# Gated recurrence: the products of k with the carried decays on GpSimd, those of q on VectorE

## The chip, the cores and the metric

One core of one Trainium2 chip runs the whole program. The metric is the device time of one execution in microseconds (us). The kernel before took 1620.99 us, the median of three runs (1618.9 to 1622.72).

## The reference, cut to what matters

The program is two blocks of two layers each in fp32, on 256 tokens and a width of 1024. The change lies in layer 0 of the second block, in a gated linear recurrence with 6 heads of 128 channels:

```python
f = lb[l] + (1.0 - lb[l]) * sigmoid(f_raw);  q = silu(q_raw);  k = 1.0 - f
# per head: S_t = diag(f_t) S_{t-1} + k_t v_t^T,   o_t = S_t^T q_t, chunkwise:
scores = einsum('bhtd,bhsd,bhtsd->bhts', q, k, decay)   # decay = exp(c_t - c_s), s <= t
o = einsum('bhts,bhsv->bhtv', scores, v) + einsum('bhtd,bhdv->bhtv', q * exp(c), state)
```

Beside it, and independent of it until the output product, the same layer attends to 256 memory tokens with 4 heads: `qm = rms_norm(split_heads(qm_raw)) * gain`, softmax of `qm km^T`, and the product with `vm`.

## The kernel before, in words

Five engines run a program each, in a fixed order that the list `schedule()` gives: every engine goes through the same list of stages and does its own part of each. They meet at semaphores: `mark(key)` counts one up when an instruction ends, and `wait_ge(*at(key))` holds the engine until that count is there. An engine works strictly in order; what stands behind a waiting instruction waits too.

The recurrence is computed without a scan, by doubling. Products with TensorE are taken at seven levels s = 1, 2, 4, ... 64. At level s the tokens fall into pairs of neighbouring blocks of s; the scores between the right block's q and the left block's k are what this level contributes. So that one plain product gives them, q carries the decay from the start of its block and k the decay to the end of its block. After each level both are carried on to blocks of 2s: the q of each right block (buffer `hX`) is multiplied by the total decay of its left neighbour, the k of each left block (buffer `hk`) by the total decay of its right neighbour. The totals (`spans`) are ready before the first level.

One level (`("hg_level", s)`) goes thus:

- TensorE, `st_hg_level` (L1434): waits for `("hX", s)`, then 12 head-chunks of scores into three PSUM banks, marked `("hl", s, 0..2)`. All matmuls are recorded at L804 (the helper `mm`).
- VectorE, `st_hg_level` (L2701): waits for `("hl", s, 2)`, since it overwrites what TensorE has just read, then `carry(s)` (L2676): one product for q (L2681), one for k (L2682), each 128 x 768 elements, in place; the mark `("hX", 2s)` is on the second of them. At the last level each has 128 x 384 elements (L2686, L2687). Then six masked copies (L2717) put the three banks' scores into `ST`.
- GpSimd had no part in it.

Between the levels the list puts other work of the layer, `fill[s]`, ahead of `hg_level(s)`: projections `("pa", ...)`, which need about 6 us of TensorE, before levels 2, 4, 8 and 32; the normalisation of the memory queries, `("memq", 0)`, ahead of the projection before level 8; the scores of the memory attention, `("att", "e0", 0)` before level 16 and `("att", "e0", 1)`, with `("sm", "e0", 0)`, before level 32; and transposes and the product with v, `("pt", "e0", 0)` and `("pv", "e0", 0)`, before level 64.

`memq` goes over four engines: ScalarE evacuates the projected queries, GpSimd squares them (L2818, 128 x 512), TensorE sums the squares with a product against ones (the first instruction of TensorE's part, in front of the projection `("pa", "i", 2)`), ScalarE takes the inverse root, VectorE scales (L2620). In the list `memq` stands directly behind `hg_level(4)`.

The memory attention's softmax is VectorE's row maximum (`st_att`, L2397, L2402), ScalarE's exponentials, VectorE's reciprocal and scaling (`st_sm`, L2412, L2415), then TensorE's transposes (`st_pt`, L1186). In VectorE's order these stand between the levels: `att e0 0`, `hg_level(16)`'s carry comes after it, and `att e0 1` and `sm e0 0` behind that.

Weights arrive by DMA from the SP queue; ScalarE and VectorE split each weight into a high part and a rest (L1518, L2075) for TensorE. These splits stand in the same stages.

Of the kernel before, what the change touches and what calls it, by code (L numbers as in the profile page):

```python
# [19 lines left out]
ALU = mybir.AluOpType  # L20
# [3 lines left out]
P = 128  # L24
S = 256
# [7 lines left out]
H_H = 6  # L33
# [3 lines left out]
LEVELS = [1, 2, 4, 8, 16, 32, 64]  # L37
# [315 lines left out]
def two_blocks(nc, w, out, old):  # L353
# [46 lines left out]
    with ctx:  # L400
# [7 lines left out]
        def at(key):  # L408

            return old.at[key] if old.at else ("counting", 1)  # L410

        def sb(name, shape, dtype=F32):
            return ctx.enter_context(nc.sbuf_tensor(name, shape, dtype))
# [22 lines left out]
        def C(name, rows=P):  # L436
            a, b = CONST[name]
            return const[0:rows, a:b]
# [14 lines left out]
        def view(*dims, at=None, parts=False):  # L453
            n = int(np.prod(dims))
            if at is None:
                at = top[0]
                top[0] += n
                assert top[0] <= ARENA, top[0]
            v = (arena_parts if parts else arena)[:, at:at + n]
            names = "abcd"[:len(dims)]  # L460
            if len(dims) > 1:
                v = v.rearrange(f"p ({' '.join(names)}) -> p {' '.join(names)}", **dict(zip(names[1:], dims[1:])))
            return v
# [48 lines left out]
        hh, hl = (sb(n, [P, 2, 2, S], F32R) for n in ("hidden_high", "hidden_rest"))  # L512
# [21 lines left out]
        spans = view(6 * S)  # L534
        hk = view(6, S)
        kf = view(6, S, at=top[0])
        vf = view(NT, 768, at=top[0] + 6 * S)
        hE = view(6, S)
        hX = view(6, S)
# [87 lines left out]
        def bcast(ap, n):  # L627
            return ap.unsqueeze(2).to_broadcast([ap.shape[0], ap.shape[1], n])

        def over(ap, n):  # L630
            return ap.unsqueeze(1).to_broadcast([ap.shape[0], n, ap.shape[1]])
# [130 lines left out]
        def _(eng):  # L762
            pe = Steps(eng, "pe", sems, new)
# [39 lines left out]
            def mm(o, a, b, first=True, last=True):  # L803
                return eng.matmul(o, a, b, start=first, stop=last)  # L804
# [600 lines left out]
                ins.then_inc(*pe.mark(st))  # L1405

            def st_hg_kdT(st):
                pe.wait_ge(*at(("hX", P)))
                for g, (a, n) in enumerate(((0, 4), (4, 2))):
                    b = group(("kdT", g))  # L1410
                    for h in range(n):
                        ins = eng.transpose(b[:, h * P:h * P + P], hk[:, a + h, 0:P], ident)
                    ins.then_inc(*pe.mark(("kdT", g)))
# [20 lines left out]
            def st_hg_level(st):  # L1434
                s = st[1]
                pe.wait_ge(*at(("hX", s)))
                for g in range(3):
                    b = group(("hl", s, g))
                    for i in range(4):
                        n, h = divmod(4 * g + i, 6)  # L1440
                        if s == LEVELS[-1]:
                            ins = mm(b[0:64, i * P + 64:i * P + P], hk[:, h, n * P:n * P + 64], hX[:, h, n * P + 64:n * P + P])
                            continue
                        for d in (0, 64):
                            c = n * P + d
                            ins = mm(b[d:d + 64, i * P + d:i * P + d + 64], hk[:, h, c:c + 64], hX[:, h, c:c + 64])
                    ins.then_inc(*pe.mark(("hl", s, g)))
# [610 lines left out]
        def _(eng):  # L2058
            dv = Steps(eng, "dve", sems, new)
            TTs, TS, STT = eng.tensor_tensor, eng.tensor_scalar, eng.scalar_tensor_tensor  # L2060
# [615 lines left out]
            def carry(s):  # L2676

                left, right = totals(s)
                (kl, _), (_, qr_) = halves(hk, s), halves(hX, s)
                if s < LEVELS[-1]:  # L2680
                    TTs(qr_, qr_, bcast(left, s), ALU.mult).then_inc(*dv.mark())  # L2681
                    TTs(kl, kl, bcast(right, s), ALU.mult).then_inc(*dv.mark(("hX", 2 * s)))  # L2682
                    return
                by_head = lambda v: v.rearrange("p (h n) -> p h n", h=H_H)
                q, k = hX[:, :, P + s:S], hk[:, :, 0:s]
                TTs(q, q, bcast(by_head(left)[:, :, 1], s), ALU.mult).then_inc(*dv.mark())  # L2686
                TTs(k, k, bcast(by_head(right)[:, :, 0], s), ALU.mult).then_inc(*dv.mark(("hX", 2 * s)))  # L2687

            def st_hg_d(st):
                for g in range(3):  # L2690
# [68 lines left out]
        @block.gpsimd  # L2759
        def _(eng):  # L2760
            po = Steps(eng, "pool", sems, new)
            po.stage("init")
            eng.memset(small[:, 510:511], EPS).then_inc(*po.mark())
            po.wait_ge(*po.last())
            eng.memset(small[:, 511:512], float(-0.5 * np.log(128.0))).then_inc(*po.mark())
            po.wait_ge(*po.last())
            eng.memset(small[:, 509:510], float(-np.log(8.0))).then_inc(*po.mark())
            po.wait_ge(*po.last())
            eng.memset(lf, 0.0).then_inc(*po.mark(("consts",)))
            po.wait_ge(*po.last())  # L2770
            eng.memset(cin[:, :, 0:3], 0.0).then_inc(*po.mark(("pads", 0)))
            po.wait_ge(*po.last())
            eng.wait_ge(sems("const_in"), 16)
            T = eng.tensor_tensor
            for st in sched:
                kind = st[0]
                po.stage(kind, st)
                if kind == "norm" and st[1] == "n1":
                    po.wait_ge(*at(("outp_x", "h0")))
                    eng.memset(cin[:, :, 0:3], 0.0).then_inc(*po.mark(("pads", 1)))  # L2780
                    po.wait_ge(*po.last())
                elif kind == "l2":
                    _, l, half = st
                    for p in (2 * half, 2 * half + 1):
                        po.wait_ge(*at(("silu", l, p // 2)))
                        if p >= 2:
                            po.wait_ge(*at(("l2", l, p - 2)))
                        c = cq[:, 2 * p:2 * p + 2, :]
                        T(sq[:, p % 2], c, c, ALU.mult).then_inc(*po.mark(("sq", l, p)))
                        po.wait_ge(*po.last())  # L2790
                elif kind == "mla_norm":
                    l = st[1]
                    for j in range(2):
                        po.wait_ge(*at(("mqkv", l, "mq", j)))
                    po.wait_ge(*at(("mqkv", l, "mkv", 0)))
                    T(qp, mqkv, mqkv, ALU.mult).then_inc(*po.mark(("msq", l, 0)))
                    po.wait_ge(*po.last())
                elif kind == "gdn_a" :
                    _, l, n = st
                elif kind == "tri":  # L2800
                    _, l, n, s = st
                    po.wait_ge(*at(("AT", l, n)))
                    if s == 2:
                        po.wait_ge(*at(("T", l, n, 1)))
                    elif s > 1:
                        po.wait_ge(*at(("U", l, n, s // 2)))
                    else:
                        po.wait_ge(*at(("lhs", l)))
                    T(AM[:, n], AT[:, n], over(C(f"level{s}"), 4), ALU.mult).then_inc(*po.mark(("AM", l, n, s)))
                elif kind == "memke":  # L2810
                    l = st[1]
                    po.wait_ge(*at(("kmr", l)))
                    T(sq2[:, 0], km, km, ALU.mult).then_inc(*po.mark(("mksq", l)))
                    po.wait_ge(*po.last())
                elif kind == "memq":
                    l = st[1]
                    po.wait_ge(*at(("qmr", l)))
                    T(sq2[:, 1], qm, qm, ALU.mult).then_inc(*po.mark(("mqsq", l)))  # L2818
                    po.wait_ge(*po.last())
                elif kind in ("fox_q", "fox_k"):  # L2820
                    z = kind[-1]
                    buf = qf if z == "q" else kf
                    for p in st[1:]:
                        po.wait_ge(*at(("pb" if z == "q" else "pk", z, "raw", p)))
                        if p >= 2:
                            po.wait_ge(*at((f"f{z}n", p - 2)))
                        elif z == "q":
                            po.wait_ge(*at(("mqn" if p else "mkn", 1)))
                        c = buf[:, 2 * p:2 * p + 2, :]
                        T(sq2[:, p % 2], c, c, ALU.mult).then_inc(*po.mark((f"f{z}sq", p)))  # L2830
                        po.wait_ge(*po.last())
# [27 lines left out]
```

## Time and profile before

| | |
|---|---|
| median of 3 runs | 1620.99 us (1618.9 to 1622.72) |
| profiled execution | 1624.74 us, its span 1623.0 us |
| TensorE matmul busy | 1563.7 us, 96% of the span |
| VectorE busy | 1126.3 us, 69% |
| ScalarE busy | 890.7 us, 55% |
| GpSimd busy | 67.4 us, 4%, 58 instructions |
| mean granted TensorE clock | 0.986 of full speed |

The profiled execution took 1.74 us more than its span, from the first to the last instruction, and 3.75 us more than the median of the runs. PE is TensorE, DVE VectorE, ACT ScalarE and POOL GpSimd. A row of a timeline gives start and duration in us, engine, line and operation, output and input, and in brackets how long the engine sat idle before it and on whom it waited. The levels of the recurrence lie between 787 and 838 us of the span.

### The profile page before, as it was taken

How to read it: one execution, taken by the hardware profiler on the slowest of the kernel's cores; microseconds unless marked ns; L12 is line 12 of the kernel's file. 1: busy time of each engine (PE TensorE's matmuls, PEld its weight loads, DVE VectorE, ACT ScalarE, POOL GpSimd, SP SyncE). 2: the span in 40 equal slices, each digit the busy share in tenths (PEclk: the TensorE clock that was granted, in tenths of full speed). 3: DMA queues.
4: the chain of work that ended last, by engine and by line, in shares of the span. 5: the costliest groups of instructions: out<-in, count | busy, mean ns of one | idle time of the engine just before them, and what ended most of it. 6: DMA issues, size and time to landing. Idle time of an engine off the chain costs nothing.

```text
span 1623.0 us, 25818 instructions
## 1 busy us (share of the span) xinstructions
PE 1563.7 (96%) x10654; PEld 1374.6 (85%) x10654; DVE 1126.3 (69%) x1759; ACT 890.7 (55%) x1413; POOL 67.4 (4%) x58
## 2 busy tenths in 40 slices
PE   7999999999999999999989999989999999899999
PEld 7999877989877788889987888878888898678887
DVE  6987665798765866765776766656666666776665
ACT  5886564696564645446446544445454456654442
POOL 0113000022100000000000000000000000000000
PEclk9999989999999999999999999999999999999999
DMA  7535225544324565555424555644655553246652
GB/s 234 182 97 166 84 79 154 171 140 123 105 67 154 183 219 185 187 169 183 148 79 130 180 184 186 199 136 137 218 191 182 182 178 110 78 157 194 194 182 103
DMA packets 203621, 252.62 MB, mean 156 GB/s; under 512 B 17136, under 2 KB 183280, under 8 KB 203376
## 3 DMA queue, kind: packets, MB, share of 16 engines
q1 hardware_dynamic: 203504, 250.97, 48.4%
q8 instruction: 84, 1.38, 0.4%
q14 instruction: 33, 0.27, 0.1%
HBM read 249.90 MB, written 1.05 MB: 155 GB/s over the span
## 4 chain that ended last, share of the span: by engine, by line
PE 82%; DVE 9%; ACT 6%; DMA 1%; issue 1%; SPq 0%; POOL 0%; DVEq 0%; ACTq 0%; POOLq 0%
PE bank L804 80%; ACT arena L1518 3%; DVE weights_rest L2075 2%; ACT weights_high L1518 1%; DMA ring<-in_w_in 1%; DVE arena L2223 1%; PE bank L1186 1%; DVE xT L2469 1%; DVE weights_rest_more L2075 1%; DVE small L2397 0%; ACT L1513 0%; PE bank L861 0%; DVE x L2438 0%; DVE arena L2717 0%; SPq L736 0%
## 5 line engine op out<-in xcount | busy, mean ns | idle before, releaser
L804 PE MATMUL bank<-xT,weights_high 128*128 128x256 f32 (+2 forms) x3152 | 699.5, 332 | 7.8 <-DVE weights_rest L2075 3.9
L2075 DVE TENSOR_TENSOR weights_rest<-ring,weights_high 128x1024 fp32r<-128x1024 f32 (+2 forms) x410 | 481.9, 1219 | 230.5 <-ACT weights_high L1518 228.9
L804 PEld LDWEIGHTS bank<-xT,weights_high 128*128 128x128 f32 (+1 forms) x3152 | 515.0, 191 | 48.0 <-issue 7.1
L1518 ACT ACTIVATE weights_high<-ring 128x1024 fp32r<-128x1024 f32 (+2 forms) x410 | 399.3, 1025 | 228.1 <-PE bank L804 210.7
L804 PE MATMUL bank<-xT,weights_rest 128*128 128x256 f32 (+1 forms) x1928 | 417.3, 283 | 0.0
L804 PEld LDWEIGHTS bank<-xT,weights_rest 128*128 128x128 f32 (+1 forms) x1928 | 327.1, 190 | 19.2
L1518 ACT ACTIVATE arena<-bank 128x512 f32<-128x512 f32 (+6 forms) x236 | 112.5, 501 | 161.3 <-PE bank L804 150.1
L804 PE MATMUL bank<-arena 128*64 128x64 f32 (+5 forms) x2040 | 143.1, 258 | 7.5 <-ACT arena L1518 6.2
L804 PEld LDWEIGHTS bank<-arena 128*64 128x64 f32 (+2 forms) x2040 | 120.6, 157 | 28.6 <-issue 12.4
L1518 ACT ACTIVATE arena<-arena 128x256 f32<-128x256 f32 (+2 forms) x128 | 72.3, 565 | 113.1 <-DVE arena L2585 111.7
L804 PE MATMUL bank<-weights_high,arena_parts 128*128 128x512 f32 (+1 forms) x416 | 116.0, 382 | 2.3 <-DVE small L2402 2.3
L2075 DVE TENSOR_TENSOR weights_rest_more<-ring_more,weights_high 128x1024 fp32r<-128x1024 f32 x68 | 81.0, 1232 | 47.5 <-ACT weights_high L1518 47.2
L804 PE MATMUL bank<-weights_high,xT 128*128 128x256 f32 (+1 forms) x384 | 98.9, 346 | 7.8 <-DVE xT L2469 3.6
L2585 DVE TENSOR_REDUCE arena<-bank 128x256 f32<-128x512 f32 x160 | 102.5, 682 | 0.0
L804 PE MATMUL bank<-weights_high,hidden_high 128*128 128x512 f32 x352 | 100.0, 391 | 0.0
L804 PE MATMUL bank<-weights_high,hidden_rest 128*128 128x512 f32 x352 | 99.4, 389 | 0.0
L1518 ACT ACTIVATE weights_high<-ring_more 128x1024 fp32r<-128x1024 f32 x68 | 68.4, 1057 | 50.6 <-PE bank L804 50.5
L804 PEld LDWEIGHTS bank<-weights_high,arena_parts 128*128 128x128 f32 x416 | 76.5, 192 | 16.6 <-DVE small L2402 2.5
L804 PEld LDWEIGHTS bank<-weights_high,xT 128*128 128x128 f32 x384 | 65.1, 190 | 19.8 <-issue 5.5
L804 PEld LDWEIGHTS bank<-weights_high,hidden_high 128*128 128x128 f32 x352 | 66.1, 188 | 14.4
L804 PEld LDWEIGHTS bank<-weights_high,hidden_rest 128*128 128x128 f32 x352 | 66.1, 188 | 14.2
L804 PE MATMUL bank<-weights_rest,hidden_high 128*128 128x512 f32 x272 | 75.6, 389 | 0.0
(187 smaller groups left out, 1563.8 us busy)
## 6 DMA issues: line engine op xcount, KB each, us to landing
ring<-in_w_in SPq DMA_DIRECT2D x36, 1024.0 KB, 5.3
ring<-in_ffn_w_gate SPq DMA_DIRECT2D x71, 512.0 KB, 4.1
ring<-in_ffn_w_up SPq DMA_DIRECT2D x71, 512.0 KB, 5.1
ring<-in_ffn_w_down SPq DMA_DIRECT2D x34, 1024.0 KB, 4.9
ring<-in_w_out SPq DMA_DIRECT2D x22, 1024.0 KB, 4.9
ring<-in_w_in_a SPq DMA_DIRECT2D x11, 1024.0 KB, 5.3
ring_more<-in_ffn_w_down SPq DMA_DIRECT2D x10, 1024.0 KB, 4.9
ring_more<-in_ffn_w_gate SPq DMA_DIRECT2D x17, 512.0 KB, 4.0
```

The source lines that it names most:

```text
L804: return eng.matmul(o, a, b, start=first, stop=last)
L1186: ins = eng.transpose(b[:, c:c + P], pb[:, t, f, kt * P:kt * P + P], ident)
L1518: return eng.activation(dst, src, func, **kw_)
L2075: TTs(rest_slot(b)[:, part], raw_slot(b)[:, part], high_slot(key)[:, part].bitcast(F32), ALU.subtract).then_inc(*dv.mark(("rest", key, z)))
L2223: STT(out=cq[:, i, :], in0=cin[:, i, j:j + S], scalar=taps[:, j:j + 1], in1=cq[:, i, :], op0=ALU.mult, op1=ALU.add).then_inc(*dv.mark(*((( ...
L2469: STT(out=xl[:, k, to], in0=src, scalar=g, in1=xh[:, k, to].bitcast(F32), op0=ALU.mult, op1=ALU.subtract).then_inc(*dv.mark(("xl", id, t, ...
L2585: eng.tensor_reduce(dst, v.rearrange("p a b -> p b a"), AX, ALU.add).then_inc(*dv.mark(*keys, frees=g))
```

## The change

The product for k leaves VectorE's `carry` and is issued by GpSimd, in the same stage `("hg_level", s)` of its list. It has a mark of its own, `("hK", 2s)`, and TensorE waits for it beside `("hX", 2s)` at the next level, and at the transposes of k (`st_hg_kdT`). GpSimd waits for the same three things as VectorE (the scores of the level, the totals, and k itself), does its one product, and waits for its end before it goes on.

```diff
             def st_hg_kdT(st):
-                pe.wait_ge(*at(("hX", P)))
+                pe.wait_ge(*at(("hK", P)))
...
             def st_hg_level(st):
                 s = st[1]
                 pe.wait_ge(*at(("hX", s)))
+                if s > 1:
+                    pe.wait_ge(*at(("hK", s)))
...
                 if s < LEVELS[-1]:
-                    TTs(qr_, qr_, bcast(left, s), ALU.mult).then_inc(*dv.mark())
-                    TTs(kl, kl, bcast(right, s), ALU.mult).then_inc(*dv.mark(("hX", 2 * s)))
+                    TTs(qr_, qr_, bcast(left, s), ALU.mult).then_inc(*dv.mark(("hX", 2 * s)))
                     return
...
+                elif kind == "hg_level":
+                    s = st[1]
+                    po.wait_ge(*at(("hk",)))
+                    po.wait_ge(*at(("hl", s, 2)))
+                    po.wait_ge(*at(("spans", LEVELS[-1])))
+                    at_ = 6 * S - 12 * S // s
+                    total = hE.rearrange("p a b -> p (a b)") if s == 1 else spans[:, at_:at_ + 6 * S // s]
+                    right = total.rearrange("p (n z) -> p n z", z=2)[:, :, 1]
+                    if s < LEVELS[-1]:
+                        k = hk.rearrange("p a b -> p (a b)").rearrange("p (n z s) -> p n z s", z=2, s=s)[:, :, 0, :]
+                        T(k, k, bcast(right, s), ALU.mult).then_inc(*po.mark(("hK", 2 * s)))
+                    else:
+                        k, by_head = hk[:, :, 0:s], right.rearrange("p (h n) -> p h n", h=H_H)
+                        T(k, k, bcast(by_head[:, :, 0], s), ALU.mult).then_inc(*po.mark(("hK", 2 * s)))
+                    po.wait_ge(*po.last())
```

## Rows read from the trace of the kernel before

**Rows 1.** The page, part 1: busy time, share, instructions.
```profile
PE 1563.7 (96%) x10654; PEld 1374.6 (85%) x10654; DVE 1126.3 (69%) x1759; ACT 890.7 (55%) x1413; POOL 67.4 (4%) x58
```

**Rows 2.** Timeline of PE: start, duration, operation, idle before, releaser.
```profile
804.90 1.62 PE L804 MATMUL bank<-arena 128*64 128x64 f32 x48
807.17 1.12 PE L804 MATMUL bank<-arena,const 128*128 128x512 f32 x2 [0.65 <-POOL arena L2818]
...
813.97 2.68 PE L804 MATMUL bank<-arena 128*64 128x64 f32 x56
817.51 1.62 PE L804 MATMUL bank<-arena 128*64 128x64 f32 x48 [0.86 <-DVE arena L2682]
819.51 1.13 PE L804 MATMUL bank<-arena 64*128 64x256 f32 x8 [0.38 <-DVE arena L2717]
...
829.83 1.38 PE L1186 MATMUL bank<-const,arena 128*128 128x128 f32 x8 [1.69 <-DVE arena L2415]
833.31 4.50 PE L804 MATMUL bank<-arena 128*64 128x128 f32 x40 [2.10 <-ACT arena L1518]
```

**Rows 3.** Timeline of DVE over the levels.
```profile
806.57 1.36 DVE L2681 TENSOR_TENSOR arena<-arena 128x768 f32<-128x768 f32 x1 [0.39 <-PE bank L804]
...
815.63 0.96 DVE L2681 TENSOR_TENSOR arena<-arena 128x768 f32<-128x768 f32 x1 [0.77 <-PE bank L804]
816.51 0.95 DVE L2682 TENSOR_TENSOR arena<-arena 128x768 f32<-128x768 f32 x1
817.49 2.83 DVE L2717 COPY_PREDICATED arena<-const,bank 64x256 f32<-64x256 uint32 x6
820.35 0.76 DVE L2397 TENSOR_REDUCE small<-bank 128x1 f32<-128x256 f32 x2
...
822.34 0.96 DVE L2681 TENSOR_TENSOR arena<-arena 128x768 f32<-128x768 f32 x1
...
829.16 0.62 DVE L2415 TENSOR_SCALAR arena<-arena,small 128x256 f32<-128x256 f32 x2
...
829.89 0.62 DVE L2415 TENSOR_SCALAR arena<-arena,small 128x256 f32<-128x256 f32 x2
```

**Rows 4.** Timeline of POOL over the whole span.
```profile
64.14 3.88 POOL L2789 TENSOR_TENSOR arena<-arena 128x512 f32<-128x512 f32 x2
...
113.15 1.27 POOL L2809 TENSOR_TENSOR arena<-arena,const 128x512 f32<-128x512 f32 x1 [19.39 <-issue]
...
806.07 1.04 POOL L2818 TENSOR_TENSOR arena<-arena 128x512 f32<-128x512 f32 x1 [51.46 <-ACT arena L1518]
...
1097.33 1.04 POOL L2830 TENSOR_TENSOR arena<-arena 128x512 f32<-128x512 f32 x1 [7.92 <-ACT arena L1518]
```

**Rows 5.** The chain that ended last, around memq: start, duration, what.
```profile
805.01 0.61 ACT arena L1518
...
805.65 0.42 issue
```

**Rows 6.** Timeline of DVE where POOL was at work.
```profile
113.13 0.69 DVE L2305 TENSOR_TENSOR arena<-bank,arena 128x512 f32<-128x512 f32 x1
113.74 1.24 DVE L2310 TENSOR_TENSOR arena<-arena 128x512 f32<-128x512 f32 x1
...
1097.34 1.06 DVE L2631 TENSOR_SCALAR small<-small 128x24 f32<-128x24 f32 x1
1098.44 0.18 DVE L2081 TENSOR_SCALAR small<-small 128x24 f32<-128x24 f32 x1
```

**Rows 7.** Timeline of PE after a long gap, at another place.
```profile
274.81 1.48 PE L841 MATMUL bank<-const,arena 128*128 128x128 f32 x8 [3.32 <-DVE arena L2489]
```

**Rows 8.** Busy time by stretch, then granted clock (PEclk), DMA share, GB/s.
```profile
274.00:277.00 3.00, 2.14 (x11) 1.74 (x12) 2.36 (x7) 3.00 (x7) 0.00 (x0) 0.73 0.77 268
277.00:280.00 3.00, 3.00 (x21) 3.00 (x20) 3.00 (x7) 2.44 (x5) 0.00 (x0) 0.70 0.00 0
...
834.00:838.00 4.00, 4.00 (x38) 3.88 (x35) 3.65 (x9) 1.56 (x2) 0.00 (x0) 0.50 0.02 4
```

More of the change, by code:

```diff
@@ L2680, in carry @@
                 if s < LEVELS[-1]:
-                    TTs(qr_, qr_, bcast(left, s), ALU.mult).then_inc(*dv.mark())
-                    TTs(kl, kl, bcast(right, s), ALU.mult).then_inc(*dv.mark(("hX", 2 * s)))
+                    TTs(qr_, qr_, bcast(left, s), ALU.mult).then_inc(*dv.mark(("hX", 2 * s)))
                     return
                 by_head = lambda v: v.rearrange("p (h n) -> p h n", h=H_H)
-                q, k = hX[:, :, P + s:S], hk[:, :, 0:s]
-                TTs(q, q, bcast(by_head(left)[:, :, 1], s), ALU.mult).then_inc(*dv.mark())
-                TTs(k, k, bcast(by_head(right)[:, :, 0], s), ALU.mult).then_inc(*dv.mark(("hX", 2 * s)))
+                q = hX[:, :, P + s:S]
+                TTs(q, q, bcast(by_head(left)[:, :, 1], s), ALU.mult).then_inc(*dv.mark(("hX", 2 * s)))
             def st_hg_d(st):
```

## The prediction, made before the changed kernel was run

> **What bounds the kernel now.** I read the page's busy times first: TensorE's matmuls fill 96% of the span, GpSimd is busy 4% of it [rows 1]. So VectorE's time is worth something only where TensorE waits for it, and the question is where it waits between 787 and 838 us. The timeline of TensorE answers that: in each row the bracket says how long it stood still and for whom [rows 2]. It goes from the scores of levels 2 and 4 into a projection or out of one without a gap, so the carries of levels 1, 2 and 4, and that of 16, are ready before they are asked for: behind a projection of some 6 us a carry of 1.9 us is hidden. It stands still five times: 0.65 us before the memory queries' norm (for GpSimd), 0.86 us before level 16 (for VectorE's product of k, L2682), 0.38 us for a bank that L2717 frees, 1.69 us before the transposes at 829.83 (for VectorE's L2415), 2.10 us before 833.31 (for ScalarE, which follows these transposes) [rows 2]. The timeline of VectorE shows why: from 815.63, when the scores of level 8 end, to 830.5, the end of the second pair of L2415, it works almost without a pause, two carries within [rows 3].
>
> **The change part by part.** All times are those of the profiled execution, 1624.74 us with a span of 1623.0 us, 3.75 us above the median of the runs; I carry the difference over to that median.
>
> VectorE loses seven products, of which two, at levels 8 and 16, lie on its chain to L2415. Each is 0.95 us by itself, 0.87 us from start to the next start [rows 3].
>
> GpSimd gains them. No row shows it at 128 x 768 with runs of s elements. Its 128 x 512 takes 1.04 us with both inputs the same buffer and 1.27 us with two, one of them broadcast [rows 4]. In proportion 768 elements take 1.56 or 1.91 us; the dearest row, two of 512 in 3.88 us, which holds waits, would give 2.91 us. I take 1.9 us, from the row with two inputs and a broadcast, and keep 1.56 and 2.9. The Trainium skill (GPSIMD Engine Reference, § 3.1) puts a two-input product at about 2.6 cycles an element at 1.2 GHz, which as an estimate is 1.66 us; by it the sum below would be 3.2 + 1.7 - 1.3 = 3.6 us, since the pair that is spoken of at the end of it would then just escape.
>
> GpSimd's product does not run beside VectorE's of q. Where both work from SBUF they take turns: VectorE's 512 elements at 113.74 took 1.24 us beside a GpSimd product that lasts to 114.42, but the one with an input from PSUM at 113.13 took its 0.69 us beside the same one; at 806.57 L2681 took 1.36 instead of 0.96 us, beside GpSimd's of 806.07; a tiny L2631 took 1.06 us beside the one of 1097.33, where the next scalar operation took 0.18 [rows 3, 4, 6]. Released by TensorE, VectorE starts within 0.05 us; GpSimd, released at 805.62, spent 0.42 us on issue and began at 806.07 [rows 4, 5]. So q goes first: with t the end of a level's scores, q runs to t + 0.97, k from there to t + 2.87. Before, both were done at t + 1.85 or so: k comes a microsecond later. Behind a projection that costs nothing.
>
> The masked copies (L2717) read the mask from SBUF and the scores from PSUM, like the undisturbed instruction at 113.13; I take them as undisturbed, and as the other bound let each turn cost them a product of GpSimd. The Trainium skill (SBUF — State Buffer, § Who interferes with whom) says the same of the products, that with two inputs in SBUF the later of the two engines waits for the whole instruction; it adds that a VectorE instruction with at most one SBUF input does not contend. By that rule the masks stay free and the sum stands.
>
> *The memory queries' norm.* This is the costly place. GpSimd is in order, and in its list `hg_level(4)` stands in front of `memq`. Until now it squared the queries from 806.07 to 807.11, and TensorE took them at 807.17 [rows 2, 4]. Now it waits for the scores of level 4, which end at 806.52 [rows 2], and works off k first. VectorE's q: 806.57 to 807.54. k: to 809.44. The squares, 0.06 us behind it (a wait on its own end): 809.50 to 810.54. TensorE begins at 810.59 instead of 807.17: 3.42 us. Nothing covers that: TensorE's next instruction in order is that product with ones, and the 6 us projection `("pa", "i", 2)` stands behind it. With 1.56 us for k it is 3.1, with 2.9 it is 4.4, with masks in turn 0.45 more. Without taking turns k would run from 807.0 to 808.9 and the delay would be 2.85 us.
>
> *The clock.* TensorE then has stood still for 4 us, after 806.52. After a gap of 3.32 us at 274.81 the granted clock was 0.73 and 0.70 in two stretches of 3 us, that is 3.4 us at 1.2 GHz (0.27 x 3 / 0.5 + 0.30 x 3 / 0.5) [rows 7, 8]. After 0.65 or 0.86 us the clock stays. I count one such spell, which falls into a projection that keeps TensorE full: half of 3.4 us, 1.7 us. It could be nothing, or, as after the gaps of 1.69 and 2.10 us, a spell twice as long, 3.4 us [rows 2, 8].
>
> *From level 8 on*, with t = 0 at the end of its scores (815.61 before). TensorE begins level 16 when k is there, at 2.90 instead of 1.90, so the scores of level 16 end at 4.52 instead of 3.52. The bank wait of 0.38 us goes (VectorE's masks end at 3.80). The projection (5.95 us) and level 32 follow: TensorE is at the transposes at 13.17 instead of 12.54. VectorE, one product lighter, ends the masks at 3.80 and the maxima at 5.82. GpSimd's k of level 16 has begun at 4.97 and holds the q of level 16 up until 6.87; q to 7.75, masks to 10.6, maxima to 12.6, first pair of L2415 12.82 to 13.44 (before 13.55 to 14.17). That is early enough for TensorE. But GpSimd's k of level 32 is ready to start at 13.62 (13.17 + 0.45) just when the second pair is issued, and holds it up: k to 15.52, the pair to 16.14, instead of 14.90. What hangs on that pair, TensorE's second transposes and ScalarE's part behind it [rows 2], comes 1.25 us later than before. With k at 1.56 us the pair is through before k is ready, and it comes 1.35 us earlier; with 2.9 us it is even; with masks that take turns 2.0 us later.
>
> Levels 1, 2 and 64 cost nothing: a projection follows each (at 64 the k of 384 elements is asked for only at the transposes of k, some 7 us on). Behind 838 us everything waits on TensorE's order and moves with it. DMA is not touched.
>
> Sum: 3.42 + 1.7 + 1.25 = 6.4 us. Against the median: 1620.99 + 6.4 = 1627.4 us. By the bounds: least 3.1 - 1.35 + 0 = 1.7, most 3.9 + 3.4 + 2.0 = 9.3 us, so 1622.7 to 1630.3 us for this case.
>
> **The rivals.** First, *VectorE's relief pays*: of the 1.69 us before the transposes and the 0.38 us all goes, and with them the spell at 1.2 GHz that follows. In it 40 matmuls took 4.50 us [rows 2, 8], at full clock half of that, so 2.25 us are to be had; in all 4.3 us. It decides for faster as soon as memq costs TensorE less than 4.3 us, clock included. For it: the chain from 815.63 to 830.5 is VectorE's. Against it: the second product takes its turns from the same chain. With k at 1.56 us, no spell, and no turns (2.5 us at memq) it gives -1.8 us, 1619.2 us; further down memq would have to wait less than 1 us, as if k were put off behind it. Chance of this side 0.08, 0.05 of it beyond what can be measured.
>
> Second, *a draw*: the delay at memq is there, but the clock stays or is given back at 831 us, and the second pair escapes k. 3.42 - 1.35 = 2.1 us, 1623.1 us. For it: the pair and k meet within a few tenths of a microsecond. Against it: every gap above 2 us that I looked at has a spell behind it. Chance 0.2.
>
> Third, *GpSimd is slow on short runs*: at 4 us for k memq costs 5.5, the spell 2.5, and level 16 adds a wait of 3.1 us, of which the DVE chain gives 2 back at the transposes: 9 us, 1630 us. For it: no row has runs of 1 to 32 elements. Against it: a broadcast and a stride have cost 0.23 us so far. Chance 0.06.
>
> **How the numbers follow.** The forecast has 0.66. What a measurement can tell from no change is about 0.2%, 3.2 us. The slower side is the third rival and the forecast but for its lowest part (0.02): 0.06 + 0.64 = 0.70. Within 0.2%: the draw, that part, and 0.03 of the first rival: 0.25. Faster: 0.05. The range reaches from 1621.0, below the draw, to 1633.0, above the third rival and the run-to-run scatter of 2 us.
>
> **What would show it.** Right: GpSimd's k about 1.9 us plus its wait, seven times; the squares of memq at about 809.5; TensorE's gap before the product with ones about 4 us instead of 0.65, its releaser GpSimd; a stretch after it at half clock; level 16 waiting for GpSimd by 1.8 us. Wrong: the squares still near 806, or a gap there under 2 us; q and k side by side at full speed; the 1.69 us at the transposes gone and with it the slow spell at 831.

## The result, and the profile after

The changed kernel took 1628.07 us, median of 5 runs (1627.66 to 1629.32), beside 1620.41 us for the kernel before, now also of 5: a ratio of 1.0049, 95% interval 1.0034 to 1.0063, so 5.5 to 10.2 us slower. Forecast were 6.4 us more and 1627.4 us. In a second set of runs the ratio was 1.0036 (1.0024 to 1.0049). The profiled executions, 1624.74 us before and 1629.32 us after, differ by 4.6 us.

The page's first part shows that the work did move: GpSimd has seven instructions and 13.8 us more, VectorE seven fewer and 4.2 us less [rows 1].

```profile
PE 1564.5 (96%) x10654; PEld 1375.8 (85%) x10654; DVE 1122.1 (69%) x1752; ACT 890.7 (55%) x1413; POOL 81.2 (5%) x65
```

Next the timeline of TensorE after, where [rows 2] stand before; a row is start, duration, operation, and the idle time before it. The first one is the start of the stretch that is compared below.

```profile
787.53 4.39 PE L804 MATMUL bank<-arena 128*128 128x128 f32 x72
...
805.30 1.62 PE L804 MATMUL bank<-arena 128*64 128x64 f32 x48
810.58 2.08 PE L804 MATMUL bank<-arena,const 128*128 128x512 f32 x2 [3.66 <-POOL arena L2833]
819.87 2.68 PE L804 MATMUL bank<-arena 128*64 128x64 f32 x56
824.05 2.68 PE L804 MATMUL bank<-arena 128*64 128x64 f32 x56 [1.50 <-DVE arena L2717]
832.60 1.62 PE L804 MATMUL bank<-arena 128*64 128x64 f32 x48
836.33 1.84 PE L1186 MATMUL bank<-const,arena 128*128 128x128 f32 x8 [2.11 <-DVE arena L2417]
840.27 3.91 PE L804 MATMUL bank<-arena 128*64 128x128 f32 x40 [2.10 <-ACT arena L1520]
```

The gap before the product with ones is 3.66 us instead of 0.65, its releaser GpSimd. That product itself takes 2.08 us instead of 1.12, and the 6.8 us from its start to the scores of level 8 have become 9.3 us: half clock. The gap before level 16 is 1.50 instead of 0.86 us; the row names L2717, but that is a mask which ended at about the same time as GpSimd's k (821.65 + 2.26 = 823.91). In the run with the gap filled, told below, the same wait of 1.50 us names GpSimd's k. The bank wait of 0.38 us is gone: the scores of level 16 and those of the attention now stand in one row (x56).

GpSimd's timeline has all the new products (L2820, the last one L2823) and the squares of memq (L2833):

```profile
792.50 2.54 POOL L2820 TENSOR_TENSOR arena<-arena 128x768 f32<-128x768 f32 x1 [37.48 <-PE bank L804]
799.58 2.59 POOL L2820 TENSOR_TENSOR arena<-arena 128x768 f32<-128x768 f32 x1 [4.53 <-PE bank L804]
807.07 2.33 POOL L2820 TENSOR_TENSOR arena<-arena 128x768 f32<-128x768 f32 x1 [4.91 <-PE bank L804]
809.48 1.04 POOL L2833 TENSOR_TENSOR arena<-arena 128x512 f32<-128x512 f32 x1
821.65 2.26 POOL L2820 TENSOR_TENSOR arena<-arena 128x768 f32<-128x768 f32 x1 [11.12 <-PE bank L804]
825.81 1.52 POOL L2820 TENSOR_TENSOR arena<-arena 128x768 f32<-128x768 f32 x1 [1.91 <-PE bank L804]
834.37 1.49 POOL L2820 TENSOR_TENSOR arena<-arena 128x768 f32<-128x768 f32 x1 [7.04 <-PE bank L804]
844.33 1.15 POOL L2823 TENSOR_TENSOR arena<-arena 128x384 f32<-128x384 f32 x1 [8.46 <-PE bank L804]
```

VectorE's timeline shows the other side of the same turns: q first (806.96), the masks undisturbed beside k (2.79 us), and two scalar operations that wait for a k, at 826.17 (1.19 us, where the same one at 828.18 takes 0.17) and at 834.34 (1.93 us for the pair, where the next pair takes 0.62):

```profile
806.96 0.96 DVE L2683 TENSOR_TENSOR arena<-arena 128x768 f32<-128x768 f32 x1 [1.26 <-PE bank L804]
807.95 2.79 DVE L2717 COPY_PREDICATED arena<-const,bank 64x256 f32<-64x256 uint32 x6
...
826.17 1.19 DVE L2404 TENSOR_SCALAR small<-small 128x2 f32<-128x2 f32 x1
827.39 0.75 DVE L2399 TENSOR_REDUCE small<-bank 128x1 f32<-128x256 f32 x2
828.18 0.17 DVE L2404 TENSOR_SCALAR small<-small 128x2 f32<-128x2 f32 x1
...
834.34 1.93 DVE L2417 TENSOR_SCALAR arena<-arena,small 128x256 f32<-128x256 f32 x2
836.38 0.62 DVE L2417 TENSOR_SCALAR arena<-arena,small 128x256 f32<-128x256 f32 x2
```

Busy time by stretch, the granted clock in the third column from the right, before and then after:

```profile
808.00:811.00 3.00, 3.00 (x26) 2.87 (x24) 2.84 (x6) 2.61 (x4) 0.00 (x0) 1.00 0.46 183
811.00:814.00 3.00, 3.00 (x28) 2.87 (x26) 2.93 (x6) 2.01 (x2) 0.00 (x0) 1.00 0.00 0
```
```profile
808.00:811.00 3.00, 0.42 (x1) 0.43 (x2) 2.58 (x6) 0.00 (x0) 2.44 (x2) 0.70 0.56 228
811.00:814.00 3.00, 3.00 (x10) 1.97 (x10) 0.00 (x0) 1.31 (x2) 0.00 (x0) 0.50 0.02 5
814.00:817.00 3.00, 3.00 (x19) 3.00 (x19) 1.43 (x3) 2.94 (x4) 0.00 (x0) 0.66 0.00 0
```

After the change TensorE's clock was at 1.2 GHz for (0.30 + 0.50 + 0.34) x 3 / 0.5 = 6.8 us, of which the first part lay in the gap; before, it was at full speed there.

### The profile page after: what moved, and what is told of

It is laid out like the page before. It is cut to its first block, busy times and chain, and to the rows that moved or that the text cites. A ratio compares the mean times of both kernels' runs of the same rounds, so it can differ in the third digit from the quotient of the medians.

```text
span 1627.5 us, 25831 instructions
## 1 busy us (share of the span) xinstructions
PE 1564.5 (96%) x10654; PEld 1375.8 (85%) x10654; DVE 1122.1 (69%) x1752; ACT 890.7 (55%) x1413; POOL 81.2 (5%) x65
## 3 DMA queue, kind: packets, MB, share of 16 engines
q8 instruction: 84, 1.38, 0.3%
## 4 chain that ended last, share of the span: by engine, by line
PE 79%; DVE 10%; ACT 7%; issue 1%; DMA 1%; SPq 0%; POOL 0%; DVEq 0%; ACTq 0%; POOLq 0%
PE bank L804 77%; ACT arena L1520 4%; DVE weights_rest L2077 3%; ACT weights_high L1520 2%; DMA ring<-in_w_in 1%; DVE arena L2225 1%; PE bank L1186 1%; ACT L1515 1%; DVE xT L2471 1%; DVE weights_rest_more L2077 0%; DVE small L2399 0%; PE bank L861 0%; ACT L1520 0%; DVE x L2440 0%; PE bank L841 0%
```

## The experiments

All are told against the kernel before, run beside them; the first four are one set, the last four another. Since whole executions of one kernel scatter by some 7 us (1616.5 to 1623.3 us in 29 of the kernel before), the timelines are compared in one stretch, from the row of 72 matmuls that holds the scores of level 1 to the first weights of the output product (862.20 before, 868.20 after). Its five pieces, in us, end at memq's product with ones, at the scores of level 16, at the softmax's transposes, at the product with v (p v), and at the output product. Each runs from the start of one TensorE row to the start of the next; the second and third are given as one where nothing marks the start of level 16. A line of the table is one profiled execution, but for the ratio, which is that of the times of all executions to those of the kernel before:

| kernel | to memq | to level 16 | to the transposes | to p v | to the output | sum | ratio, 95% interval |
|---|---|---|---|---|---|---|---|
| before | 20.03 | 10.34 | 12.32 | 3.48 | 28.89 | 75.06 | |
| changed | 23.05 | 13.47 | 12.28 | 3.94 | 27.93 | 80.67 | 1.0049 (1.0034 to 1.0063) |
| changed, second set | 23.04 | 12.46 | 12.28 | 3.94 | 28.08 | 79.80 | 1.0036 (1.0024 to 1.0049) |
| memq first | 19.71 | 10.97 | 12.29 | 3.48 | 28.80 | 75.25 | 0.9999 (0.9990 to 1.0008) |
| only k of level 4 on VectorE | 19.71 | 10.98 | 12.29 | 3.48 | 27.83 | 74.29 | 1.0006 (0.9995 to 1.0017) |
| busy gap | 23.05 | 10.98 | 12.30 | 3.48 | 27.97 | 77.78 | 1.0024 (1.0013 to 1.0035) |
| without q at level 4 | 22.34 | 10.97 | 12.28 | 3.49 | 27.84 | 76.92 | one execution |
| memq first, k32 on VectorE | 19.70 | 10.98 | 10.97 | 3.48 | 28.11 | 73.24 | 0.9994 (0.9985 to 1.0003) |
| the same, k16 too | 19.70 | 10.98 | 10.81 | 3.48 | 28.08 | 73.05 | 0.9991 (0.9983 to 0.9999) |
| memq first, no k at 8 to 32 | 19.70 | 20.94 | | 3.49 | 26.46 | 70.59 | 0.9989 (0.9979 to 0.9999) |

**Memq first.** GpSimd squares the memory queries ahead of its k of level 4:

```diff
-            for st in sched:
+            order = list(sched)
+            order.remove(("memq", 0))
+            order.insert(order.index(("hg_level", 4)), ("memq", 0))
+            for st in order:
```

Expected: 

> GpSimd squares the memory queries ahead of its product of k at level 4; all seven products of k stay on GpSimd. Theory (the loss is the queue in front of memq and the slow clock behind it): the squares are back near 806.4 us, TensorE's gap before the product with ones falls from 3.66 to about 0.7 us, no stretch at half clock between 809 and 816, and some 5.5 of the 7.7 us are gone: about 1622.5 us (1621 to 1624.5), with the gap of 2.1 us at the transposes still there. Rival (the turns that GpSimd and VectorE take on SBUF are the loss, spread over seven levels): the order of two GpSimd instructions changes little, 1626 to 1628 us.

Measured: 1621.26 us, ratio 0.9999 (0.9990 to 1.0008). All seven products are still on GpSimd, and nothing of the loss is left that can be measured. The gap at memq is 0.32 us, even less than before:

```profile
803.18 1.12 PE L804 MATMUL bank<-arena,const 128*128 128x512 f32 x2 [0.32 <-POOL arena L2836]
814.15 2.68 PE L804 MATMUL bank<-arena 128*64 128x64 f32 x56 [1.50 <-DVE arena L2717]
826.44 1.38 PE L1186 MATMUL bank<-const,arena 128*128 128x128 f32 x8 [2.12 <-DVE arena L2417]
```

The loss hangs on the order of two GpSimd instructions. The waits that the turns make further on are all there (1.50 and 2.12 us), as in the changed kernel, and the stretch is only 0.2 us longer than before: the rival, which put the loss on the turns, falls. The theory had left some 2 of the 7.7 us to them; that was too much.

**Only k of level 4 back on VectorE.**

```diff
+                    if s in (4,):
+                        TTs(kl, kl, bcast(right, s), ALU.mult).then_inc(*dv.mark(("hK", 2 * s)))
...
-                elif kind == "hg_level":
+                elif kind == "hg_level" and st[1] not in (4,):
```

Expected: 

> Only the product of k at level 4 goes back to VectorE; the other six stay on GpSimd. Theory: nothing stands in front of memq any more, so the same as with memq first, about 1622.5 us (1621 to 1624.5). Rival (turns): one product in seven is undone, so about one seventh of the loss comes back, 1627 us.

Measured: 1621.94 us, ratio 1.0006 (0.9995 to 1.0017). One of the seven products carries the loss, and this is the one in front of memq; a seventh of it is not what came back.

**The gap filled.** Three more products of TensorE stand before the wait of memq:

```diff
+                if l == 0:
+                    for _ in range(3):
+                        mm(b[:, :], C("ones64"), C("tri"))
                 pe.wait_ge(*at(("mqsq", l)))
```

Expected: 

> The changed kernel with three more products of TensorE (128x512, of constants, into the bank that memq then overwrites) in the gap before the product with ones, some 3.4 us of work that fills it. Theory (standing still lowers the clock, and that costs about 2.5 us): memq begins as late as in the changed kernel (810.6), but the clock stays at 1.0 between 809 and 816, and the time falls to about 1625.5 us (1624.5 to 1626.5). Rival (only the wait costs, the clock falls for another reason or costs nothing): 1628 us or a little more.

Measured: 1625.26 us, ratio 1.0024 (1.0013 to 1.0035). In the stretch memq begins as late as in the changed kernel (23.05 us in both), and the piece behind it is 10.98 instead of 13.47 us. The three products took 2.84 us and left a gap of 0.90 us:

```profile
805.61 2.84 PE L804 MATMUL bank<-const 128*128 128x512 f32 x6
809.34 1.12 PE L804 MATMUL bank<-arena,const 128*128 128x512 f32 x2 [0.90 <-POOL arena L2836]
```

and the clock, by stretch, stayed at full:

```profile
807.00:810.00 3.00, 2.10 (x7) 0.80 (x5) 2.35 (x6) 0.00 (x0) 2.21 (x2) 1.00 0.48 195
810.00:813.00 3.00, 3.00 (x25) 2.76 (x24) 0.00 (x0) 2.46 (x3) 0.00 (x0) 1.00 0.02 5
```

TensorE did more work and the stretch got shorter, by 2.9 us against the first profile of the changed kernel and by 2.0 against the second. The times of whole executions point the same way, though the intervals touch (1.0013 to 1.0035 against 1.0034 to 1.0063) or overlap (1.0024 to 1.0049 in the second set). Nor is the full clock behind a short gap a chance of this one execution: it stayed at 1.00 behind the wait of 1.5 us before level 16 in all eight profiles that have this wait. So standing still is what lowered the clock at memq, and the lower clock cost 13.47 - 10.98 = 2.5 us in the first profile.

**Level 4 without VectorE's q.** `carry(4)` returns at once, and nobody waits for its mark.

Expected: 

> The changed kernel without VectorE's product of q at level 4 (left out, so the scores from level 8 on are not the reference's). Theory (q goes first, and k waits for the whole of it): GpSimd's k of level 4 takes 1.5 instead of 2.33 us, the squares begin some 0.85 us earlier, TensorE's gap is about 2.8 instead of 3.66 us. Rival (2.3 us is GpSimd's own time with runs of 4 elements): k takes 2.3 us and the gap stays at 3.6 us.

Measured in one execution: GpSimd's k of level 4 took 1.63 us instead of 2.33, and TensorE's gap is 2.96 us instead of 3.66.

```profile
801.47 1.63 POOL L2824 TENSOR_TENSOR arena<-arena 128x768 f32<-128x768 f32 x1 [4.90 <-PE bank L804]
803.17 1.04 POOL L2837 TENSOR_TENSOR arena<-arena 128x512 f32<-128x512 f32 x1
```
```profile
804.27 1.13 PE L804 MATMUL bank<-arena,const 128*128 128x512 f32 x2 [2.96 <-POOL arena L2837]
```

So 0.70 us of the 2.33 were the wait for q, and both moved by the same; by itself k takes 1.63 us at this level, a little more than the 1.5 expected. The time of the whole, 1619.88 us, is that of one execution in which the clock did not fall behind memq; it says nothing on the sizes.

**Memq first, k of level 32 on VectorE.** The edits of the first two experiments, with `(32,)` in place of `(4,)`.

Expected: 

> Memq first in GpSimd's list, and the product of k at level 32 back on VectorE. Theory (at the transposes GpSimd's k of level 32 holds the scaling by VectorE up): the first pair of scalings takes 0.62 instead of 1.93 us, TensorE's gap before the transposes falls from 2.1 to about 0.8 us, and the time is some 1.3 us below that of memq first: ratio to the kernel before about 0.999 (1620 us). Rival (what VectorE loses there it has elsewhere): the gap stays at 2 us and the time at that of memq first.

Measured: 1620.16 us, ratio 0.9994 (0.9985 to 1.0003). The gap before the transposes and the scalings in front of it, TensorE and then VectorE:

```profile
824.71 1.38 PE L1186 MATMUL bank<-const,arena 128*128 128x128 f32 x8 [0.80 <-DVE arena L2417]
```
```profile
824.03 0.62 DVE L2417 TENSOR_SCALAR arena<-arena,small 128x256 f32<-128x256 f32 x2
824.76 0.62 DVE L2417 TENSOR_SCALAR arena<-arena,small 128x256 f32<-128x256 f32 x2
```

The pair takes 0.62 instead of 1.93 us and the gap 0.80 instead of 2.12, as expected; the stretch is 2.0 us shorter than with memq first. Of these, 1.3 us are the gap; the other 0.7 lie in the last piece, where the slow spell behind the transposes lasted 3.4 us by the granted clock instead of 6.8, and the 40 matmuls took 4.09 instead of 4.50 us. The times of whole executions tell this version neither from memq first nor from the kernel before.

**K of level 16 on VectorE too.** `(16, 32)`.

Expected: 

> As the one with memq first and k at level 32 on VectorE, and k at level 16 on VectorE too. Theory (k at level 16 on GpSimd spares VectorE 0.87 us and stops it for 1.0 us at a small scalar operation): no difference, the gap before the transposes 0.7 to 1.0 us, about 1620 us. Rival (relief of VectorE is what counts): a gap 0.9 us longer than with k at level 16 on GpSimd.

Measured: 1619.52 us, ratio 0.9991 (0.9983 to 0.9999), the only version with nothing left out whose interval lies below the kernel before, by 1.5 us (0.2 to 2.8) and only just; from the version above its time can't be told. The gap before the transposes is 0.63 us: not longer, as the rival had it, but 0.17 shorter. What GpSimd took off VectorE at level 16 it took back at the small scalar operation (1.19 us instead of 0.17).

**No k at levels 8, 16 and 32.**

Expected: 

> Memq first, and the products of k at levels 8, 16 and 32 left out on both engines (the result is then not the reference's): the most that taking them off VectorE could bring. Theory: TensorE's gap before level 16 goes (1.5 us), the transposes come some 2.4 us earlier than with memq first, and the time is 2 to 3 us below the kernel before (ratio 0.998 to 0.999): the prize was smaller than the 3 us that memq's wait costs. Rival (VectorE's relief is worth more, with the clock): 4 us or more below, ratio under 0.9975.

Measured: 1618.82 us, ratio 0.9989 (0.9979 to 0.9999), 1.8 us below the kernel before (0.2 to 3.4). The transposes come 20.94 us after memq instead of 23.26 with memq first, 2.3 us earlier. That is the most that relief of VectorE could give here: by its middle value less than the 3 us that memq's wait costs, by the upper end of its interval about as much. In the profiled execution the slow spell behind the transposes was gone, as the first rival had it:

```profile
824.11 1.38 PE L1186 MATMUL bank<-const,arena 128*128 128x128 f32 x8 [0.84 <-DVE arena L2417]
827.60 2.46 PE L804 MATMUL bank<-arena 128*64 128x128 f32 x40 [2.10 <-ACT arena L1520]
```

The 40 matmuls took 2.46 instead of 4.50 us, and the stretch is 4.5 us shorter than before. Of such a prize, seen in one execution, the times of all twelve leave 1.8 us.

**The changed kernel again**, unaltered, beside the last three.

Expected: 

> The changed kernel on this chip, beside the three others, to size the clock's part: its time above memq first is the wait at memq (3.3 us) and the slow clock behind it. Theory: 5.5 to 8 us above memq first, so 2 to 4.5 us of it by the clock, with a spell at half clock behind memq in the profile. Rival (the clock costs nothing): 3.3 us above.

Measured: 1627.4 us, ratio 1.0036 (1.0024 to 1.0049), so 6.0 us above the ratio of memq first, which is from the other set. Here the spell behind memq was shorter:

```profile
805.00:808.00 3.00, 2.52 (x11) 2.04 (x12) 0.63 (x2) 1.36 (x2) 0.43 (x1) 0.81 0.03 5
808.00:811.00 3.00, 3.00 (x19) 3.00 (x18) 1.48 (x3) 2.94 (x4) 0.00 (x0) 0.62 0.00 0
```

(0.19 + 0.38) x 3 / 0.5 = 3.4 us, as the prediction had taken it from the gap of 3.32 us [rows 7, 8], and it cost 12.46 - 10.98 = 1.5 us.

## Why the prediction was right

*The queue in front of memq* was the mechanism, and its price near: the product with ones came 3.02 us later in the stretch (23.05 against 20.03), where 3.42 were forecast. The order q, k, squares, and the turns, stand in the rows and in the run without q. The term was too large since k was: 1.63 us by itself at level 4, 1.52 and 1.49 us at levels 16 and 32, not 1.9. The low bound, in proportion to the row with one buffer for both inputs (1.56), was the better one. The rate in the Trainium skill (GPSIMD Engine Reference, § 3.1) had given an estimate of 1.66 us, which is nearer to the 1.5 to 1.6 us measured than 1.9 is. That the product with ones begins at 810.58 us, where 810.59 was forecast, is luck: the trace after stands 0.39 us later at the start of the stretch.

*The clock* was the second term: 1.7 us forecast, 2.5 us in one profile and 1.5 us in the other, after the same gap of 3.66 us. The run with the gap filled shows the cause. By the medians it may be more: from the ratio of the changed kernel to that of the busy gap 1.2 to 2.5 thousandths, 2 to 4 us. The intervals don't settle that more closely; what the gap costs is different from execution to execution, and only a band for it can be given.

*From level 8 on*, 1.25 us was too much. Level 16 waits 0.64 us longer (1.50 us in all, where 1.8 were forecast), as k is shorter than assumed. GpSimd's k of level 32 did hold the scalings of the softmax up, by 1.3 us, but the first pair and not the second; TensorE was at the transposes 0.6 us later. Two things in that step were wrong. K of level 16 did not stop VectorE's q, which came later (828.38), but the small scalar operation before it, for 1.0 us.

The slow spell behind the transposes was in both kernels' profiles, 6.8 us long by the granted clock; after the change it began in the transposes and not behind them. So they took 1.84 instead of 1.38 us, but the 40 matmuls 3.91 instead of 4.50: in the table the piece to p v is 0.5 us longer and the last one 1.0 shorter (0.8 in the second profile).

So in the place of 3.42 + 1.7 + 1.25 = 6.4 us the first profile has 3.0 at memq, 2.5 for the clock behind it, 0.6 at level 16 and -0.5 behind the transposes, 5.6 us in all; the second has 3.0, 1.5, 0.6 and -0.4, 4.7 us. The third term, 1.25 us, was the one that was far out: 0.1 and 0.2 us stand in its place. Behind the stretch the first profile is 1.5 us shorter than that of the kernel before (759.3 against 760.8 us to the end), where its clock stayed, as the last section shows; that leaves the 4.6 us between the profiled executions.

The times of whole executions differ by 7.7 us (second set 5.8), 2.1 (1.1) us more than the stretch. No trace shows where that rest lies. The profiled execution of the kernel before is 3 to 4 us above its medians, so its stretch may be longer than is usual, and the second one of the changed kernel (1625.06 us) is 2.3 us below its own; whether that accounts for the rest was not tried. That 6.4 us lies between the two measured differences is thus partly luck, while memq's wait and the clock behind it are shown.

*Masks beside k* took 2.79 to 2.91 us for six, as before (2.83): the bound in which they take turns is out. The Trainium skill (SBUF — State Buffer, § Who interferes with whom) has VectorE instructions with at most one SBUF input free, outside the two-port performance modes, and the trace agrees for the masks. The prediction left out that condition. The scalings, which read one tensor and a column of factors, did wait for k (1.93 instead of 0.62 us); no run here shows in which mode they ran.

*The rivals.* VectorE's relief was worth 1.8 us (0.2 to 3.4) even with no k at levels 8 to 32 at all. The second pair did escape k, as the draw had it, but the first did not; and a draw came about only where memq was not behind k. GpSimd on runs of one and two elements is slower, but little: at level 1 k takes 2.05 us, from 792.99, the end of q, to 795.04, and at level 2 1.74 us, and both are hidden behind a projection.

## What to carry to other kernels

Before work goes to an engine that idles, look at what stands behind it in that engine's list: 4% busy did not make GpSimd free at the one microsecond at which TensorE waited for it. Put the instruction that a bottleneck waits for ahead of the new work; that alone undid the loss, as far as it can be measured. An engine that takes turns with another on SBUF is not free capacity either: of the 0.87 us taken off VectorE at a level, the turns took back 1.0 us at level 16 and 1.3 us at level 32.

## What had not been expected of the hardware

Equal gaps did not get equal clocks. Before the weights of the output product TensorE stood still for 2.81 us in both kernels:

```profile
862.20 0.95 PE L804 MATMUL bank<-weights_high,xT 128*128 128x512 f32 x2 [2.81 <-DVE arena_parts L2179]
```
```profile
868.20 0.70 PE L804 MATMUL bank<-weights_high,xT 128*128 128x512 f32 x2 [2.81 <-DVE arena_parts L2181]
```

Before the change the clock fell behind it, as the granted clock by stretch shows:

```profile
861.00:864.00 3.00, 1.80 (x5) 1.48 (x6) 2.75 (x4) 3.00 (x5) 0.00 (x0) 0.74 0.00 0
864.00:867.00 3.00, 3.00 (x11) 2.36 (x10) 3.00 (x4) 1.82 (x4) 0.00 (x0) 0.69 0.02 5
```

After it, it stayed:

```profile
866.00:869.00 3.00, 0.80 (x4) 0.71 (x5) 2.71 (x5) 3.00 (x5) 0.00 (x0) 1.00 0.00 0
869.00:872.00 3.00, 3.00 (x15) 2.50 (x14) 3.00 (x4) 2.83 (x5) 0.00 (x0) 1.00 0.03 5
```

Of the ten profiled executions the clock fell behind this gap (2.80 to 2.84 us) in seven and stayed in three. So a gap has a band of prices and not one: the 3.66 us at memq were followed by 6.8 us at half clock in one profile and by 3.4 in another, the 2.96 us of the run without q by none. It may be part of why single executions of one kernel differ by some 7 us. The granted clock of whole executions goes with it: in the second set the eight executions of the kernel before under 1620 us have a mean of 0.992 or 0.993, the 17 above 1621 us one of 0.990 or less. Which gaps made the difference was not tried.
